# Moving two groups of light expert jobs from behind the first group to the end of the expert loop

## The reference, cut to what matters

```python
N_EXPERTS = 64; TOP_K = 8; D_EXPERT = 256
def moe_ffn(h, router_w, router_bias, e_gate, e_up, e_down, s_gate, s_up, s_down):
    scores = jax.nn.sigmoid((h @ router_w).astype(jnp.float32))
    ...                                  # grouped top-8 of the 64 experts per token
    gates = jnp.zeros((n, N_EXPERTS), jnp.float32).at[jnp.arange(n)[:, None], idx].set(w)
    hg = jnp.einsum('nd,edf->nef', h, e_gate)
    hu = jnp.einsum('nd,edf->nef', h, e_up)
    act = jax.nn.silu(hg) * hu * gates[:, :, None].astype(h.dtype)
    routed = jnp.einsum('nef,efd->nd', act, e_down)
    shared = (jax.nn.silu(h @ s_gate) * (h @ s_up)) @ s_down
    return routed + shared
```

## Time and profile before

| what | us |
|---|---|
| median of three runs | 897.17 |
| the profiled execution, own time | 896.34 |
| its span, first to last instruction | 894.0 |
| TensorE busy | 846.1 (95%) |
| VectorE busy | 565.9 (63%) |
| ScalarE busy | 308.9 (35%) |
| data moved | 295.93 MB, 331 GB/s over the span |
| group 0 starts (its first `up`) | 369.95 |
| group 1 starts | 408.35 |
| group 3 starts | 466.10 |
| group 14 starts | 818.51 |
| group 15 starts | 844.44 |
| last job's `up` starts | 864.15 |

### The profile page before, as it was taken

How to read it: one execution, slowest core, us unless ns; L and a number is a source line. 1 busy time by engine, 2 the same in 40 slices (tenths; PEclk the granted TensorE clock), 3 DMA queues, 4 the chain that set the end, 5 groups by cost and what they waited for, 6 DMA issues and landing times.

```text
span 894.0 us, 21073 instructions
## 1 busy us (share of the span) xinstructions
PE 846.1 (95%) x7872; PEld 639.8 (72%) x7872; DVE 565.9 (63%) x1425; ACT 308.9 (35%) x588; POOL 50.5 (6%) x92
## 2 busy tenths in 40 slices
PE   4799999999999998999999999999999999999995
PEld 2599999999999997657665556656556555666662
DVE  2458888899996878537554555546546455555555
ACT  3564444344428513022322322223232232223323
POOL 2010000000000000100000000000000000000000
PEclk9899999999999999899999999999999999999999
DMA  9984556888976746899999999999999999999961
GB/s 338 344 261 157 174 170 227 274 310 272 320 261 236 242 140 261 336 372 409 396 419 411 389 415 413 418 407 414 424 414 411 422 414 409 416 418 403 419 251 49
DMA packets 92711, 295.93 MB, mean 331 GB/s; under 512 B 7718, under 2 KB 45670, under 8 KB 67659
## 3 DMA queue, kind: packets, MB, share of 16 engines
q1 hardware_dynamic: 86139, 280.55, 81.8%
q0 software_dynamic: 6016, 13.10, 3.9%
q10 hardware_dynamic: 489, 1.33, 0.4%
HBM read 300.19 MB, written 4.14 MB: 340 GB/s over the span
## 4 chain that ended last, share of the span: by engine, by line
PE 68%; DVE 17%; DMA 7%; issue 6%; ACT 1%; SPq 0%; DVEq 0%; POOLq 0%; ACTq 0%
PE psum L887 19%; PE psum L1251 8%; PE psum L891 7%; DMA xn<-h_table,idx 6%; PE psum L1249 6%; PE psum L1246 6%; PE psum L1334 5%; PE psum L1292 5%; DVE mid L1927 4%; DVE wexp_r L1800 4%; PE psum L1298 3%; PE psum L1283 3%; DMA wexp<-in_ada_w 2%; PE psum L1331 1%; PE psum L1145 1%
## 5 line engine op out<-in xcount | busy, mean ns | idle before, releaser
L887 PE MATMUL psum<-xn_r,wexp_r 128*128 128x264 f32 x1024 | 193.8, 289 | 5.9 <-DVE hT_r L1838 5.9
L887 PEld LDWEIGHTS psum<-xn_r,wexp_r 128*128 128x128 f32 x1024 | 161.7, 191 | 8.2 <-issue 7.8
L887 PE MATMUL psum<-hT_r,wexp_r 128*128 128x264 f32 x512 | 146.3, 286 | 0.0
L1800 DVE TENSOR_TENSOR wexp_r<-wexp,wexp_r 128x1024 fp32r<-128x1024 f32 x88 | 106.5, 1217 | 20.7 <-ACT wexp_r L1510 20.3
L1510 ACT ACTIVATE wexp_r<-wexp 128x1024 fp32r<-128x1024 f32 x88 | 92.3, 1054 | 57.2 <-PE psum L887 44.5
L2232 DVE SCALAR_TENSOR_TENSOR hT<-psum,gcol,hT 64x256 f32<-64x256 f32 (+2 forms) x64 | 26.4, 413 | 133.8 <-ACT hT L1673 133.1
L887 PEld LDWEIGHTS psum<-hT_r,wexp_r 128*128 128x128 f32 x512 | 97.8, 191 | 0.1
L1249 PE MATMUL psum<-wexp,mid 128*128 128x512 f32 x208 | 94.7, 599 | 1.7 <-issue 0.9
L2247 DVE TENSOR_TENSOR bc_r<-psum,xn_r 32x256 fp32r<-32x256 f32 (+2 forms) x136 | 65.9, 485 | 27.0 <-ACT xn_r L1690 15.1
L1252 PE MATMUL psum<-wexp,mid 128*64 128x256 f32 x320 | 77.3, 384 | 0.0
L1251 PE MATMUL psum<-wexp,mid 128*64 128x256 f32 x320 | 77.2, 384 | 0.0
(11 more groups left out here) (343 smaller groups left out, 1332.1 us busy)
## 6 DMA issues: line engine op xcount, KB each, us to landing
wexp<-in_e_gate SPq DMA_DIRECT2D x64, 1024.0 KB, 9.5
wexp<-in_e_up SPq DMA_DIRECT2D x64, 1024.0 KB, 11.7
wexp<-in_e_down SPq DMA_DIRECT2D x64, 1024.0 KB, 10.7
wexp<-in_w_in SPq DMA_DIRECT2D x32, 1024.0 KB, 5.9
mid<-in_ada_w SPq DMA_DIRECT2D x8, 2048.0 KB, 9.9
wexp<-in_w_branch SPq DMA_DIRECT2D x8, 1024.0 KB, 5.3
wexp<-in_ada_w SPq DMA_DIRECT2D x14, 512.0 KB, 10.8
wexp<-in_w_out SPq DMA_DIRECT2D x4, 1024.0 KB, 5.8
```

Source lines behind the costliest of these rows:

```text
L887: last = mm(out, a[x], b[y], start=start and x == y == 0, stop=stop and x == 1)
L1800: V.tensor_tensor(as_r(low(u, q)), low(u, q), as_r(high(u, q)).bitcast(F32), ALU.subtract).then_inc(S["w_lo"], 1)
```

## The change

Both pairs of light groups stand at the end: `LIGHT_FIRST` goes from 2 to 0 and `LIGHT_LAST` from 2 to 4. Groups 1 to 11 are full, groups 12 to 15 are light with the pattern 64, 32, 64, 32. `LOOP_FROM` stays 4, `LOOP_TO` goes from 12 to 10, so the loop covers groups 4 to 9 and six groups are written out behind it. The number of jobs of each size stays the same (13, 20 and 31 of 128, 64 and 32 rows).

```diff
-LIGHT_FIRST = 2
-LIGHT_LAST = 2
+LIGHT_FIRST = 0
+LIGHT_LAST = 4
...
-LOOP_FROM = LIGHT_FIRST + 2
+LOOP_FROM = 4
 LOOP_TO = LAST - LIGHT_LAST - 1
...
-            light, full_, end = ranks[:, 0:LIGHT_FIRST, :], ranks[:, LIGHT_FIRST:LIGHT_FIRST + FULL_GROUPS, :], ranks[:, LIGHT_FIRST + FULL_GROUPS:, :]
+            full_, end = ranks[:, LIGHT_FIRST:LIGHT_FIRST + FULL_GROUPS, :], ranks[:, LIGHT_FIRST + FULL_GROUPS:, :]
...
-            g.iota(light[:, :, 1:4:2], pattern=[[2, LIGHT_FIRST], [1, 2]], base=LARGE + FULL_GROUPS, channel_multiplier=0)
...
-            g.iota(light[:, :, 0:4:2], pattern=[[2, LIGHT_FIRST], [1, 2]], base=OVER_QUARTER + 2 * FULL_GROUPS, channel_multiplier=0)
...
-                for a, b, kinds in ((0, LIGHT_FIRST, ROWS_OF_LIGHT_JOB), (LIGHT_FIRST, GROUPS - LIGHT_LAST, ROWS_OF_JOB), (GROUPS - LIGHT_LAST, GROUPS, ROWS_OF_END_JOB)):
+                for a, b, kinds in ((0, GROUPS - LIGHT_LAST, ROWS_OF_JOB), (GROUPS - LIGHT_LAST, GROUPS, ROWS_OF_END_JOB)):
```

## The result

The changed kernel takes 902.45 us (four runs, 900.73 to 903.28) against 897.0 of the kernel before (four runs, 896.05 to 897.62). The ratio is 1.0061, interval 1.0046 to 1.0077. A later set of six runs gave 901.8 against 896.7, ratio 1.0064, interval 1.0051 to 1.0076. The forecast was 902.9.

What follows compares the result with a forecast made beforehand. TensorE was taken to set the pace, with the loads following. Terms 0 - 0.9 + 7.1 = +6.2 us on 896.34 gave 902.5; half of the median's 0.8 offset made it 902.9, range 898.8 to 906.

Steps and rivals of the forecast that it cites:

- TensorE sets the pace before, with the loads just behind: Expert stage before the change: TensorE never waits for expert weights, while loads follow as slots come free.
- TensorE's work: 0: All groups: the same jobs in another order, so the sum of matmul time changes by 0.
- The front: -0.9: Light-to-full boundary at group 3 goes, gaining 0.9 us; new boundary behind group 0 costs 0; together -0.9 to +1.0.
- rival 3: Groups 1 and 2: second sheet's gather lands late, a wait up to 1.9 us, giving 904.4; chance 8%.
- The lead at job 47: 15.6: Weights land 15.6 us before use as the light groups start, bounds 15.6 and 20.4; slow start adds no stock.
- Rival 1: Light groups at the end: larger lead or faster stream removes most of the wait, 896.2 us, not slower; chance 24%.
- The pace: 31.45 us a group, need 22.7: Four end light groups: stream gives one per 31.45 us, TensorE wants one per 25.93; shortfall 22.7 us, no stream reserve.
- The wait: 7.1: Late third light group and mostly group 15: TensorE waits 7.1 us for weights, shortfall 22.7 against lead 15.6.
- rival 2: Behind job 63's weights: waits halve TensorE's clock for 6.8 us, costing 3.4 more, 905.9; chance 8%.
- Written-out code: 0: Two more groups fetched as instructions instead of looped: no difference, 0 us.
- The rivals' times: Times forecast for the rival cases: 896.2 if the lead lasts, 905.9 with the clock's fall, 904.4 with a front wait.

Runs made afterwards that it cites:

- the second: Second trace, from running the changed kernel once more with nothing altered; 901.8 us, waits for weights 5.7 us.
- one kernel (10.4 to 12.2): Against the kernel before: light groups at 3, 13, 14 and 15, group 4 written out instead of looped; 899.74 us, ratio 1.003.
- another (5.9 to 7.8): Against the kernel before: light groups at 2, 3, 14 and 15 in the end's pattern, group 1 full; 896.7 us, ratio 1.0008.

## Why the prediction was right, step by step

- *TensorE sets the pace before, with the loads just behind.* Right. A sixth less to load changed nothing that can be told (0.9994).
- *TensorE's work: 0.* Right, 845.8 against 846.1.
- *The front: -0.9.* The sign was right, the size was off: -3.0 in this trace, and -2.65 in the second (groups 1 to 3 take 100.05 there). I counted only the boundary of group 3, which gave 0.55 (33.01 to 32.46), and wrote that no gain could come of the other one. Group 1 grew by 4.7 us and group 2 by 4.8 when they became full, not by the 6.0 or 6.1 that I took from groups away from the front. So 2.5 of the 3.0 lies in these two groups. Light groups are dearer there than at the end, by 2.3 us without the product; the pattern is 0.7 of that, and what makes the rest was not separated.
- *No new wait at the front (rival 3).* Half wrong, this wait came: the turn of the second sheet waits for its rows, 0.45 and 1.07 us in groups 2 and 3 (1.5 in all, 0.5 before), inside the bound of 1.9. The gain covers it.
- *The lead at job 47: 15.6.* It was 14.9, below the lower bound of 15.6. That bound was too narrow on rows at hand: in the kernel before, job 51's weights landed at 766.1 and its `up` started at 780.79, a lead of 14.7. That the slow front adds no stock was right: the lead was 22.8 at job 7, 17.7 at job 11 and 15.6 at job 15. Rival 1 is out, in this kernel.
- *The pace: 31.45 us a group, need 22.7.* Right. The landings of jobs 47 and 63 lie 867.9 - 742.1 = 125.8 us apart, 31.45 a group. The stream had no reserve; it was full in the light groups before and after. The 435 GB/s that the Trainium skill, page "DMA: Bandwidth & Descriptors", section "Where 436 GB/s comes from", gives as the fabric's ceiling are not reached here; 418 to 420 is what the light groups got.
- *The wait: 7.1.* The last two groups grew by 8.8: 22.7 - 14.9 = 7.8 of waiting, and about 1.1 of the clock. It lay where it was expected, 0.9 us in group 14 and 5.9 ahead of the first two jobs of group 15.
- *The clock (rival 2), 8%.* It happened, smaller than priced: 1.1 us and not 3.4, and on the path in one of the two traces of the changed kernel. I gave it too little chance.
- *Written-out code: 0.* Right. Groups 12 and 13 after took 25.98, and groups 10 and 11 took 31.78 and 32.07, as 12 and 13 before (31.79 and 32.07).
- *The rivals' times.* They stand on the profiled execution (896.34) without the 0.4 that the forecast of 902.9 has on top, so 0.4 belongs to each of them as well.

The sum came out at +4.65 for the profiled spans, with +6.2 forecast. Against the forecast the wait for weights was 0.6 us larger, the clock brought 1.1 that the sum did not have, the front was 2.1 cheaper, the start of group 0 lay 0.8 earlier, by chance (over all traces group 1 starts between 407.5 and 410.2), and the ten groups in the middle and the end gave 0.2 each. Errors cancelled, and that is luck. The medians lie 5.45 apart, with 902.9 - 897.17 = 5.7 forecast. The closeness of 902.9 to 902.45 is luck too: the traced execution took 900.73, and the slower ones, up to 903.28, were not traced.

## What to carry to other kernels

Where a stream of loads and an engine run at nearly the same mean pace, the order of long and short steps decides how much lead is there when the short ones come. Write down for each step what the engine takes and what the stream takes. The lead falls by the difference in every short step, and in long ones it grows only slowly (0.2 to 0.3 us a group here) and only up to what the slots hold. Put short steps where the lead is at its highest and something else stretches the time (here behind a 38 us group), and count how many the stock pays for: here two at the end were free, the third brought 1.2 us of waits and the fourth 5.6 more.

## What the runs showed of the hardware that I had not expected

- Lead comes back slowly: 0.2 to 0.3 us a group, though the stream's pace of 31.45 and TensorE's 31.95 suggest 0.5. It was 1.8 us over nine groups in one kernel (10.4 to 12.2) and 1.9 over ten in another (5.9 to 7.8).
- The granted clock fell to 0.50 for 3.4 us behind pauses of 2.1 to 3.0 us for data, with matmuls between them, in five traces. On the path it cost 1.1 us or nothing.
- 32 matmuls of the shared product cost 3.6 us in two light groups and 6.7 us in one full one. In the light groups part of them fell into time in which TensorE otherwise waits for VectorE (1.6 and 0.8 us), so their own duration is not their price.
